# A decoder step on one core: when the HBM tables are cleared, and the order of the steps in the first projections

## The reference

```python
# layer 0: chunked gMLP mixer, then a dense SwiGLU
z = gelu(rmsnorm(x) @ w_in); u, v = split(z)
v = layernorm(v, ln_g, ln_b)            # also an output
x = x + (u * (tril(w_s) @ v + b_s)) @ w_out
x = x + (silu(h @ wg) * (h @ wu)) @ wd  # h = rmsnorm(x)
# shared keys and values of layer 1: six projections of the normed x
# (for the samples joined with paged cached rows and a cached window)
# layer 1: attention with three branches (compressed, selected, window),
# then top-2-of-8 SwiGLU experts, rows grouped by expert in blocks of 128
y = rmsnorm(x)
```

## Time and profile before

| | |
|---|---|
| time, median of 3 executions | 1342.91 us (1342.4 to 1343.21) |
| the profiled execution | 1342.47 us |
| its span | 1340.7 us, 21550 instructions |
| mean granted clock of TensorE | 0.984 of 2.4 GHz |
| busy: PE, DVE, ACT, POOL | 1272.4, 1053.5, 929.6, 76.0 us |
| chain that ended last, by engine | PE 76%, DVE 10%, issue 5%, ACT 4%, SP's queue 3%, DMA 2% |
| HBM | 367.41 MB read, 27.45 MB written |

### The profile page before, as it was taken

The page is one execution under the profiler, slowest core; times in us unless marked ns, Lnnn a source line. Parts: engine busy times, 40 slices in busy tenths (PEclk is TensorE's granted clock), DMA queues, the critical chain, the costliest instruction groups (busy, mean ns, idle before and its releaser), DMA issues.

```text
span 1340.7 us, 21550 instructions
## 1 busy us (share of the span) xinstructions
PE 1272.4 (95%) x7272; PEld 1082.5 (81%) x7272; DVE 1053.5 (79%) x1552; ACT 929.6 (69%) x1378; POOL 76.0 (6%) x76
## 2 busy tenths in 40 slices
PE   6789999999985999899999999999999999999996
PEld 6789999999953778788888888888888888887874
DVE  6777666567523885699898998998998998998985
ACT  5555444456452785688887987987987888878873
POOL 1000000004210000200000000000000000002500
PEclk9999999999997999899999999999999999999998
DMA  8374444456689007599899898998998998998930
GB/s 339 127 272 174 178 174 182 184 189 252 215 323 405 2 1 302 195 416 417 343 407 385 338 419 337 383 414 324 404 405 323 416 396 331 415 390 319 410 141 33
DMA packets 59711, 391.50 MB, mean 292 GB/s; under 512 B 6686, under 2 KB 12962, under 8 KB 21186
## 3 DMA queue, kind: packets, MB, share of 16 engines
q1 hardware_dynamic: 51010, 354.29, 67.0%
q0 software_dynamic: 8640, 36.40, 7.2%
HBM read 367.41 MB, written 27.45 MB: 295 GB/s over the span
## 4 chain that ended last, share of the span: by engine, by line
PE 76%; DVE 10%; issue 5%; ACT 4%; SPq 3%; DMA 2%; DVEq 0%; ACTq 0%
PE bank L1809 16%; PE bank L1811 16%; PE bank L1810 16%; PE bank L1451 7%; PE bank L1452 6%; PE bank L1453 6%; DVE w_lo L1333 3%; SPq L422 2%; DMA win_v_past<-in_win_v 2%; DVE d_lo L950 2%; PE bank L1794 1%; PE bank L1646 1%; ACT w_hi L812 1%; ACT d_hi L596 1%; DMA ring<-in_wd 1%
## 5 line engine op out<-in xcount | busy, mean ns | idle before, releaser
L1333 DVE TENSOR_TENSOR w_lo<-raw,w_hi 128x1024 fp32r<-128x1024 f32 x528 | 622.8, 1220 | 36.3 <-ACT w_hi L812 18.8
L812 ACT CAST w_hi<-raw 128x1024 fp32r<-128x1024 f32 x528 | 543.1, 1055 | 93.4 <-PE bank L1811 92.2
L1809 PE MATMUL bank<-w_hi,xg_hi 128*128 128x512 f32 x704 | 275.0, 391 | 1.5 <-DVE w_lo L1333 1.5
L1811 PE MATMUL bank<-w_hi,xg_lo 128*128 128x512 f32 x704 | 274.4, 390 | 0.0
L1810 PE MATMUL bank<-w_lo,xg_hi 128*128 128x512 f32 x704 | 274.0, 389 | 0.0
L950 DVE TENSOR_TENSOR d_lo<-ring,d_hi 128x1024 fp32r<-128x1024 f32 x120 | 146.0, 1223 | 88.0 <-ACT d_hi L596 87.9
L1451 PE MATMUL bank<-hA_hi,d_hi 128*128 128x264 f32 x640 | 185.4, 290 | 18.6 <-DVE d_lo L950 9.6
L1452 PE MATMUL bank<-hA_lo,d_hi 128*128 128x264 f32 x640 | 182.8, 286 | 0.0
L1453 PE MATMUL bank<-hA_hi,d_lo 128*128 128x264 f32 x640 | 182.6, 285 | 0.0
L596 ACT CAST d_hi<-ring 128x1024 fp32r<-128x1024 f32 x120 | 124.8, 1043 | 66.1 <-PE bank L1453 61.9
L1809 PEld LDWEIGHTS bank<-w_hi,xg_hi 128*128 128x128 f32 x704 | 132.3, 188 | 29.4 <-DVE w_lo L1333 2.2
(11 more groups left out here) (330 smaller groups left out, 1579.5 us busy)
## 6 DMA issues: line engine op xcount, KB each, us to landing
raw<-in_moe SPq DMA_DIRECT2D x264, 1024.0 KB, 6.7
ring<-in_wd SPq DMA_DIRECT2D x29, 2048.0 KB, 8.4
out_rows<-zeros POOLq DMA_DIRECT2D x1, 6656.0 KB, 60.5
slot_rows<-zeros POOLq DMA_DIRECT2D x1, 6144.0 KB, 29.5
out_rows<-yrow POOLq DMA_DIRECT2D x8, 512.0 KB, 7.5
xs<-slot_rows POOLq DMA_DIRECT2D x7, 512.0 KB, 3.5
arena<-in_cmp_pages POOLq DMA_DIRECT2D x16, 128.0 KB, 3.3
X2v<-in_cmp_pages POOLq DMA_DIRECT2D x16, 128.0 KB, 2.6
```

The costliest lines, as they stand in the source:

```text
L812: nc.scalar.copy(w_hi[:, i % NSPLIT, :], raw[:, u % NRAW, ITEM * (i % 2):ITEM * (i % 2) + ITEM])\
L1333: V.tensor_tensor(w_lo[:, i % NSPLIT, :], raw[:, (i // 2) % NRAW, ITEM * (i % 2):ITEM * (i % 2) + ITEM], w_hi[:, i % NSPLIT, :].bitcast(F3 ...
L1809: T.matmul(out, lhs_hi, hi, start=first, stop=False)
L1811: return T.matmul(out, lhs_lo, hi, start=False, stop=last)
```

## The change

One wait is added on POOL's queue ahead of the clearing DMAs. In the first projections ScalarE casts, and VectorE subtracts, one item further ahead, VectorE's scaling of a block comes ahead of the remainder instead of behind it, and the scalings of u and the remainders of the later items are placed between the steps of the layer norm.

```diff
--- before.py
+++ after.py
@@ -519,6 +519,7 @@
             pool.wait_ge(gtok_ready, 2)
             pool.dma_start(grow[:], gsam[0:NS, :]).then_inc(grow_in, 16)
             pool.wait_ge(zeros_ready, 1)
+            pool.wait_ge(past_v_in, 16 * (NS * PAGES + 1))
             for rows in (slot_rows.rearrange("b p n -> (b p n)"), out_rows[0:NO_ROW, :].rearrange("r n -> (r n)")):
                 rows = rows.rearrange("(p q n) -> p q n", p=P, n=256)
                 pool.dma_start(rows, zeros[:].unsqueeze(1).to_broadcast(list(rows.shape))).then_inc(rows_zeroed, 16)
@@ -620,11 +621,11 @@
             std(1, 0)
 
             for c in range(KC):
-                round_to("vu", c)
+                round_to("vu", c + 1)
                 act.wait_ge(v_scaled, c + 1)
                 nc.scalar.activation(vT[:, c, :], vT[:, c, :], ACT.Gelu_apprx_tanh).then_inc(v_ready, 1)
             for c in range(KC):
-                round_to("vu", KC + c)
+                round_to("vu", KC + c + 1)
                 act.wait_ge(u_scaled, c + 1)
                 nc.scalar.activation(uT[:, c, :], uT[:, c, :], ACT.Gelu_apprx_tanh).then_inc(u_ready, 1)
                 if c in (1, 2):
@@ -970,36 +971,38 @@
                 scaled(uT[:, c, :], "vu", KC + c, u_scaled)
 
             for k in range(KC):
-                rest_to("vu", k)
                 scaled(vT[:, k, :], "vu", k, v_scaled)
+                rest_to("vu", k + 1)
                 if k:
                     add_up(vT, k - 1, v_ready, k)
             add_up(vT, KC - 1, v_ready, KC)
-            rest_to("vu", 8)
+            u_scale(0)
+            rest_to("vu", 9)
             dve.wait_ge(mean_done, 2)
             settle(V.tensor_copy(mu[:, :], STAT[:, 0:NT]))
             for k in range(KC):
                 V.tensor_tensor(vT[:, k, :], vT[:, k, :], mu[:, :], ALU.subtract).then_inc(ctr_ready, 1)
-            u_scale(0)
-            u_scale(1)
-            for k in range(KC):
-                if k == 4:
-                    u_scale(2)
-                rest_to("vu", 9 + k // 4)
+                if k == 3:
+                    u_scale(1)
+                    rest_to("vu", 10)
+            for k in range(4):
+                add_up(hB, k, csq_ready, k + 1)
+            u_scale(2)
+            rest_to("vu", 11)
+            for k in range(4, KC):
                 add_up(hB, k, csq_ready, k + 1)
             u_scale(3)
-            rest_to("vu", 11)
+            rest_to("vu", 12)
             inv_std(ln_rstd)
             for k in range(KC):
-                if k == 5:
-                    rest_to("vu", 12)
+                if k == 3:
                     u_scale(4)
+                    rest_to("vu", 13)
                 V.scalar_tensor_tensor(vT[:, k, :], vT[:, k, :], vector("lng")[:, k:k + 1], ln_rstd[:, :], ALU.mult, ALU.mult)\
                     .then_inc(ln_scaled, 1)
-            rest_to("vu", 13)
-            u_scale(5)
-            u_scale(6)
-            u_scale(7)
+            for c in range(5, KC):
+                u_scale(c)
+                rest_to("vu", 9 + c)
             for i in range(0, 6, 2):
                 r = P if i < 4 else NS
                 dve.wait_ge(vt_done, i + 1)
```

## The result

| | before | after |
|---|---|---|
| median of 7 executions each | 1342.47 us (1342.3 to 1343.43) | **1334.40 us (1328.14 to 1339.43)** |
| the profiled execution | 1342.47 us | 1328.32 us |
| its span | 1340.7 us | 1326.4 us |
| mean granted clock in it | 0.984 | 0.986 |

The ratio is 0.994, with a 95% interval of 0.9921 to 0.996: faster by 0.6%, and outside the range of 1322.3 to 1332.8 us. The kernel before keeps within 1.1 us here; the changed one spreads over 11 us. The seven times go with the mean granted clock of TensorE: 1328.14 us at 0.988, 1328.32 at 0.986, three from 1334.3 to 1335.3 at 0.980, 1337.11 at 0.975 and 1339.43 at 0.974. So there are two things to explain: the short executions, 1.3 us off the forecast, and what the others lose.

What follows compares the result with a forecast made beforehand. TensorE's matmuls on split weights were taken as the bound, so only its idle between them could go: 10.5 us at the attention's start plus 5.3 in the projections, 15.8 in all, giving 1326.9 us, range 1322.3 to 1332.8.

Steps and rivals of the forecast that it cites:

- Part one: Attention's start: clearing waits until win_v has landed; gain 10.5 us, between 9.7 and 12.
- bo0 and bo1 take nothing from win_v: Attention's start: dense tiles queued behind win_v don't share with it, so it lands in about 8.4 us.
- The earlier start: Attention's start: TensorE begins the sample values, line 1674, at 413.2 instead of 422.9 us, gaining 9.7 us.
- Part two: First projections: earlier casts and remainders shorten TensorE's waits; gain 5.3 us, bounds 3 and 8.
- The step that failed: Behind product 15: three remainders ahead of VectorE's vtok copy start the second turn 1.4 us later; net loss 0.3 us.
- signs of being right: Among them: win_v within 9 us, clearing starting near 410, mixing's first addition at 73 to 75 us instead of 80.3.
- signs of being wrong: win_v above 15 us, longer heads, ScalarE's cast waiting for the ring, or a scatter later than 536 us.
- Full clock in both spells: Rival: neither idle of about 3 us lets the clock fall, parts give 12 and 8, 1322.7 us; 15%.
- win_v sharing with bo0 and bo1: Rival at the attention's start: win_v lands at 416.8 us and TensorE keeps the low clock, 1331.4 us; 10%.
- the clearing not being what held it: Rival: win_v's 21.2 us come from HBM or SP's own queue, only 5.3 us gained, 1337.4 us; 4%.
- Part two paying nothing: Rival in the projections: ScalarE's earlier cast waits for a tile not landed, holding v's gelus; 1332.2 us; 8%.
- Slower, by the clearing under the heads: Rival: clearing traffic slows the loop over the heads; 1357 us if 50 us become 60% longer; 3%.

Runs made afterwards that it cites:

- clear_only: The kernel before with only the added wait on POOL, projections as they were: median 1331.99 us, ratio 0.9931.
- after: The changed kernel (both edits) against the kernel before, first series: median 1334.40 us, ratio 0.994; its profiled execution 1328.32 us.
- after_again: The changed kernel run once more, 12 executions: median 1334.11 us, ratio 0.9937 to the kernel before.
- after_third: The changed kernel run for one more profile, a single execution: 1333.62 us.
- proj_only: The changed kernel without the added wait on POOL, so only the projections changed: median 1345.74 us, ratio 1.002 to the kernel before.
- fill_turns: The changed kernel with unread matmuls in TensorE's idle times between the turns of tokens: median 1325.48 us, ratio 0.9878 to the kernel before.
- before_held: The kernel before with the remainders of items 16 and 17 moved ahead of VectorE's copies of vtok: median 1352.59 us, ratio 1.0049.
- fill_both: The changed kernel with unread matmuls ahead of the mean of squares and between the turns: median 1325.43 us, ratio 0.9874 to the kernel before.
- rest_behind: The changed kernel with the remainders of items 16 to 18 moved back behind VectorE's copies of vtok: median 1328.60 us, ratio 0.9903 to the kernel before.

## Why the prediction was wrong

**Part one, right in its sum, by luck: two of its terms were off and made up for each other.** Forecast 10.5 us; clear_only measured 10.7 (1342.7 to 1332.0). As forecast, win_v landed in 8.7 us (8.4), the wait of 2.9 us (3.2) is ended by VectorE's last copy, and the scatter waits for VectorE, not for the clearing. The heads showed no loss: from the first matmul of line 1674 to the scatter it is 129.3 us before and 126.8 us in clear_only and after, shorter by just what those matmuls gained. That bo0 and bo1 take nothing from win_v was hardly tested: in the changed kernel they were issued 2.4 and 7.0 us behind it. SP's issuing of the pages took 25.7 us before and 17.2 now, so win_v had even more room; it changed nothing, because VectorE's copy was next.

The earlier start is 8.2 us, not 9.7: counted from the 32 matmuls of the second transposes (at 398.30 us before and 397.25 in clear_only) the sample values start after 24.6 and 16.4 us. Of the missing 1.5 us, 1.0 is a collision that I had not looked for, here in the timelines of before and of clear_only, 397 to 414 us (line 1137 is 1138 there):

```profile
403.50 0.17 DVE L1137 TENSOR_SCALAR arena<-arena 128x3 f32<-128x3 f32 x1
```

```profile
401.36 2.23 POOL L525 DMA_DIRECT2D slot_rows<-zeros  x1 [29.91 <-DMA win_v_past<-in_win_v]
402.45 1.13 DVE L1138 TENSOR_SCALAR arena<-arena 128x3 f32<-128x3 f32 x1
403.73 0.77 PE L1621 MATMUL bank<-arena 128*128 128x128 f32 x2 [3.47 <-DVE arena L1138]
```

The new wait puts POOL's issue of the clearing beside a small step of VectorE that TensorE waits for. The step takes 1.1 us instead of 0.17 and ends with POOL's issue; in after it takes 1.3 us and ends with it too, and in after_again, where it came first, it took 0.17. The clock made up for it. The 64 matmuls of line 1674 took 6.16 us before and 3.7 in clear_only, after and after_third, at full clock, and 5.1 in after_again. Behind the idle of 2.8 to 2.9 us ahead of them the clock was 1.00 in three of these four profiles, so it gave back 2.5 us and not 0.8; 8.2 and 2.5 are 10.7.

**Part two, right in its sum for the short execution, and wrong in its last term.** In the short execution the waits went as forecast: 7.4 to 0.4 us for remainders, 2.9 us in one piece ahead of the mean of squares (3.0 forecast). Taking off the 2.1 us by which it started late, the mixing's first addition came 5.2 us earlier, for 5.3 forecast. But the pieces do not agree. From the timelines of PE and DVE, each profile counted from its first reciprocal, in us:

| piece | before | after | after_third | proj_only | fill_turns |
|---|---|---|---|---|---|
| to the mean of v | 22.4 | 20.5 | 20.5 | 20.9 | 21.0 |
| to the mean of squares | 12.8 | 12.3 | 12.3 | 12.3 | 12.3 |
| to the first turn of tokens | 18.6 | 13.7 | 13.7 | 13.8 | 13.6 |
| to the second turn | 1.7 | 3.4 | 3.4 | 3.4 | 3.4 |
| to the mixing's first addition | 5.3 | 5.8 | 6.1 | 7.0 | 4.6 |
| to the output projection's first addition | 10.0 | 10.4 | 16.7 | 17.2 | 10.4 |

Up to the first turn, that is to the end of product 15, the short execution gained 7.4 us where 5.6 were forecast (6.0 in after_again). Behind it the execution lost 2.2 us up to the mixing's first addition where 0.3 were forecast. The two errors cancel, so that the short executions (1325.5 to 1328.3) lie around 1326.9 is in part luck.

**The step that failed** is the last of part two: "the second turn of tokens starts 1.4 us later behind product 15 ... Net loss 0.3". I priced the three remainders ahead of the copy as a delay, and the clock only where it had fallen before, in product 15, with the 1.6 us of a spell that is over within that product. The idle that they make (2.3 us) lies in front of turns and mixing. Up to the output projection's first addition the step lost 1.3 us at full clock (fill_turns), 2.5 us with a short spell (after), 9.1 and 10.6 us with a long one (after_third, proj_only), although TensorE is busy through it. Why the clock comes back soon in some executions and not in others is open: the runs show the place and the trigger, not the reason. From the second turn on a long spell lasts 20 to 24 us and costs 7.9 and 9.3 us against full clock (22.8 and 24.2 us for 14.9), and 8.6 us in the old order (before_held, 23.9 for 15.3). In the 19 executions of the changed kernel in its two series (7 and 12) 13 are over 1333 us. Removing this idle by fills takes the median from 1334 to 1325.5; making it in the kernel before adds 10 us.

**The signs.** Of the signs of being right the start of the clearing (399.6 us, not 410) and the first addition (77.2 us, 75.1 without the late start, for 73 to 75) came out otherwise. Two signs of being wrong came true and were harmless: the scatter starts at 538.4 us, behind the limit of 536, 2.1 of it by the late start, and waits for VectorE's slots; and ScalarE's cast does wait for the ring, 2.0 us in after and 3.3 in fill_both, while TensorE waits for remainders at most 1.0 us in all.

**The rivals.** Full clock in both spells (1322.7): no version reached it as a median; the nearest is fill_both with 1325.4. win_v sharing with bo0 and bo1 (1331.4) and the clearing not being what held it (1337.4) fell with its landing in 8.7 us. Part two paying nothing (1332.2): proj_only paid nothing at the median, but by the clock, not by the ring of casts that I had described: in its profile the clock is 0.50 from 70 us to near 93. Why its median is even 3 us over that of before one profile does not show, for there the shorter wait for win_v (9.6 us for 12.9) takes up what the spell cost. With the turns filled the gain is there. Slower, by the clearing under the heads (1357), fell too: the heads kept their length, and the scatter starts 13.8 us earlier than in the earlier trace rows. I had a rival for both low spells staying away and none for one that grows, so the range ended at 1332.8 for reasons that had nothing to do with the clock, and the median fell 1.6 us outside it.

## What to carry to other kernels

Price an idle of TensorE by what follows it, not by its length alone: some 3 us in front of the projections' products went with a low spell of 1.6 us, 2.3 us in front of the token turns with a price of 1.2 us in some executions and of 8 to 9 in others. Work that TensorE does not wait for (here remainders for the next stage) belongs behind the copy that it does wait for. Where an order must leave such an idle, a few unread matmuls in it worked here. A background transfer should be held until the last transfer that somebody waits for has landed, and its issue kept away from steps that others wait for. And add up what a change gains stage by stage: here two sums were right with wrong terms.

## What the runs showed of the hardware that I had not expected

- The granted clock can stay at 1.2 GHz while TensorE is busy without a break: after_third from 75 to 90 us, 5.00 us of PE in each window, clock 0.50. In the same place, from the same program, it is 1.00 in other executions. The Trainium skill (TensorE: Matmul & The Clock Gate, section "Part 1: The HAM clock gate") has sustained matmul work bring the clock back; in these rows turns and mixing, busy by the profile, do not, and it is back only in the output projection behind them. Here the measurement decides.
- One program can have two kinds of executions: before_held has five times from 1341.3 to 1345.5 and seven from 1352.5 to 1355.3, nothing between, with means 9.9 us apart.
- SP's issue of the 16 value pages (line 443) took 25.7 us with the clearing in flight and 17.2 without it (23.8 in proj_only, 17.2 in clear_only), so the traffic goes with slower issuing as well as slower landing. The 16 key pages (line 434) took 22.5 us in both kernels with next to no clearing beside them, so such issues have other limits too; which, no run shows.
- A step of VectorE on 128 x 3 elements took 1.0 to 1.3 us instead of 0.17 beside POOL's issue of a DMA and ended with it (after, after_third, clear_only, rest_behind, fill_turns).
